# A two-block transformer's mixer: the operand turned without its row scale under the last unit of the feed-forward, the scale put on the columns as they leave, and two narrow products computed by feature

## The reference

```python
def rms_norm(t, g):
    y = tf * lax.rsqrt(jnp.mean(tf * tf, axis=-1, keepdims=True) + NORM_EPS)
    return (y * g)
# first block, layer l
x = x + 0.5 * swiglu(rms_norm(x, ffn1_norm[l]), ffn1_w_in[l], ffn1_w_out[l])
z = rms_norm(x, mix_norm[l]) @ mix_w_in[l]          # 3 attention column groups, 4 forget gates, RWKV columns
z_fox, z_moba, z_rwkv = split(z)
# forgetting attention: s = q k^T / 8 + c_i - c_j, c = cumsum(log_sigmoid(f + bias)), causal softmax
# RWKV: zf = zf + (z_prev - zf) * mu              # mix of a token with the one before it, by feature
#       r, k, v, w_lo, a_lo, g_lo = split(zf); low-rank products of tanh(w_lo), a_lo, sigmoid(g_lo)
# second block, layer l
p = rms_norm_2(x, norm_g[l]) @ w_in[l]              # among its columns: 64 index keys ik and 8 index weights iw
```

## Time and profile before

| | us |
|---|---|
| median of 3 runs | 1896.34 (1893.74 to 1907.27) |
| the profiled execution | 1899.43 |
| its span, first to last instruction | 1898.1 |
| PE busy | 1857.7 (98%) |
| DVE busy | 1165.2 (61%) |
| ACT busy | 927.7 (49%) |
| POOL busy | 93.6 (5%) |
| mean granted clock of TensorE | 0.991 of full speed |

### The profile page before, as it was taken

One profiled execution on the slowest core, in us unless ns is written; L12 is line 12 of the kernel. 1 busy time (PEld: TensorE's weight loads), 2 busy tenths in 40 slices (PEclk: granted clock), 3 DMA queues, 4 the chain that ended last, 5 costly groups with the idle time before them and its releaser, 6 DMA issues.

```text
span 1898.1 us, 28284 instructions
## 1 busy us (share of the span) xinstructions
PE 1857.7 (98%) x11756; PEld 1565.4 (82%) x11756; DVE 1165.2 (61%) x1645; ACT 927.7 (49%) x1409; POOL 93.6 (5%) x59
## 2 busy tenths in 40 slices
PE   7999999999999999999999989999999999999999
PEld 6888888887888888888888878888888888888887
DVE  5555477765655565554677656555588548597556
ACT  5444474234544454445642355444455554556553
POOL 0000010040000000000100400000010000000000
PEclk9999999999999999999999999999999999999999
DMA  6655442023555566554420235655554456454454
GB/s 241 249 183 175 145 156 78 25 79 112 168 189 188 177 191 248 188 176 143 155 71 25 79 111 187 205 184 174 165 168 159 152 188 210 151 166 156 161 186 141
DMA packets 83616, 299.19 MB, mean 158 GB/s; under 512 B 9632, under 2 KB 10784, under 8 KB 83232
## 3 DMA queue, kind: packets, MB, share of 16 engines
q1 hardware_dynamic: 79328, 287.87, 45.8%
q10 hardware_dynamic: 3840, 8.03, 1.2%
q0 software_dynamic: 320, 1.48, 0.2%
HBM read 296.30 MB, written 1.05 MB: 157 GB/s over the span
## 4 chain that ended last, share of the span: by engine, by line
PE 94%; DVE 4%; issue 0%; ACT 0%; DMA 0%; POOL 0%; ACTq 0%; DVEq 0%
PE ps L342 24%; PE ps L344 24%; PE ps L343 24%; PE ps L367 2%; PE ps L369 2%; PE ps L368 2%; PE ps L808 1%; PE ps L1184 1%; PE ps L566 1%; PE ps L1187 1%; DVE wlo L324 1%; PE ps L2500 1%; PE ps L1175 1%; PE ps L1587 1%; PE ps L780 1%; DVE a_lo L420 1%
## 5 line engine op out<-in xcount | busy, mean ns | idle before, releaser
L324 DVE TENSOR_TENSOR wlo<-raw,whi 128x1024 fp32r<-128x1024 f32 (+1 forms) x546 | 663.3, 1222 | 423.0 <-ACT whi L315 422.0
L315 ACT ACTIVATE whi<-raw 128x1024 fp32r<-128x1024 f32 (+1 forms) x546 | 573.0, 1053 | 512.2 <-PE ps L344 468.2
L342 PE MATMUL ps<-whi,a_hi 128*128 128x512 f32 x1696 | 677.0, 399 | 5.8 <-DVE a_lo L1874 1.8
L344 PE MATMUL ps<-whi,a_lo 128*128 128x512 f32 x1696 | 663.8, 391 | 0.0
L343 PE MATMUL ps<-wlo,a_hi 128*128 128x512 f32 x1696 | 662.8, 391 | 0.0
L342 PEld LDWEIGHTS ps<-whi,a_hi 128*128 128x128 f32 x1696 | 320.2, 189 | 76.0 <-DVE a_lo L1874 2.3
L344 PEld LDWEIGHTS ps<-whi,a_lo 128*128 128x128 f32 x1696 | 319.7, 189 | 68.7
L343 PEld LDWEIGHTS ps<-wlo,a_hi 128*128 128x128 f32 x1696 | 320.5, 189 | 62.8
L342 PE MATMUL ps<-whi,h_hi 128*128 128x512 f32 x320 | 124.9, 390 | 0.0
L344 PE MATMUL ps<-whi,h_lo 128*128 128x512 f32 x320 | 124.6, 389 | 0.0
L343 PE MATMUL ps<-wlo,h_hi 128*128 128x512 f32 x320 | 124.5, 389 | 0.0
(11 more groups left out here) (317 smaller groups left out, 1847.3 us busy)
## 6 DMA issues: line engine op xcount, KB each, us to landing
raw<-stream SPq DMA_DIRECT2D x546, 512.0 KB, 3.4
arena<-rows ACTq DMA_DIRECT2D x2, 1026.0 KB, 12.6
arena<-mem ACTq DMA_DIRECT2D x2, 1024.0 KB, 8.7
arena<-lora ACTq DMA_DIRECT2D x2, 768.0 KB, 6.1
arena<-rows ACTq DMA_DIRECT2D x2, 512.0 KB, 4.9
const_tables<-consts POOLq DMA_DIRECT2D x1, 901.0 KB, 4.9
arena<-band POOLq DMA_DIRECT2D x1, 544.0 KB, 4.0
x_res<-x SPq DMA_DIRECT2D x1, 512.0 KB, 3.7
```

Of the source, the lines that this page charges most:

```text
L315: self.split_hi.mark(act.activation(self.weights(self.whi, u), self.weights(self.raw, u), ACT.Copy), u)
L324: self.split_lo.mark(dve.tensor_tensor(self.weights(self.wlo, u), self.weights(self.raw, u), self.weights(self.whi, u).bitcast(F32), ALU.s ...
L342: pe.matmul(out, a_h, hi, start=start, stop=False, skip_group_check=True)
L344: last = pe.matmul(out, a_l, hi, start=False, stop=True, skip_group_check=True)
```

## The change

1. The feed-forward ahead of the mixer now ends as the others do: four pieces are turned unscaled before its last unit, the others between the first two low units. The diagonals and L846 are gone. The first low unit waits for the first tile of `x_done` (bank 1 is being emptied).
2. The row scale is spread over partitions by PE (`pe_mix_spread`, two matmuls into bank 2) and copied by ACT to a tile R. DVE multiplies the low-rank columns and the k, r, v columns with R on their way from PSUM to a tile ZR (which is E2), and the mixes by ACT and DVE read ZR. The attention columns get the scale in the copies they had.
3. The forget gates become features 64 to 67 of the third block: 12 matmuls per unit go, two small transposes behind `pe_rw_lora` come.
4. The index keys of the second block run by feature: 8 x 3 products with 256 moving columns in place of 48 with 72, a copy by ACT, two transposes behind the first unit of `k`, two copies with the scale.
5. In the second tile's forgetting scores the last of the cumulative matmuls leaves out the first 128 columns, where it added zeros.

```diff
     def pe_unit_turned(self, n, blocks, beside=()):
...
-            for out, c, w, first, t in beside:
-                pe.matmul(out, a_h, hi, ...); pe.matmul(out, a_h, lo, ...); pe.matmul(out, a_l, hi, ...)
...
-    def pe_mix_turn(self, l):
+    def pe_mix_spread(self, l):
+        pe.wait_ge(*self.rstd(("mix", l)))
+        pe.wait_ge(*self.x_done(l, "ffn1", 1))
         for t in range(NT):
+            ins = pe.matmul(self.bank(2)[:, t * P:(t + 1) * P], self.rs(0, t).to_broadcast([P, P]), self.c("ident"),
+        self.rw_pe.mark(ins, "rms", l)
+    def act_mix_spread(self, l):
+        act.wait_ge(*self.rw_pe("rms", l))
+        self.rw_act.mark(act.activation(self.R, self.bank(2, S), ACT.Copy), "rms", l)
...
     def dve_rw_low(self, l):
+        dve.wait_ge(*self.rw_act("rms", l))
+            m.mark(dve.tensor_tensor(self.ZR[0:w, i, :], src, self.R[0:w, :], ALU.mult), "scaled", "low", l, i)
+            dve.wait_ge(*self.rw_act("low", l, i))
+            m.mark(dve.scalar_tensor_tensor(y, self.ZR[0:w, i, 0:S - 1], ...), "low", l, i)
+    def dve_rw_scale(self, l, name, unit, bank):
+        dve.wait_ge(*self.unit_used(unit))
+        self.rw_dve.mark(dve.tensor_tensor(self.ZR, src, self.R.unsqueeze(1).to_broadcast([P, 4, S]), ALU.mult),
...
     def pe_mix(self, l):
-        self.pe_mix_turn(l)
         for n in range(4):
             self.pe_rw_low(l, n)
+            if n < 2:
+                self.pe_turn_x(("mix", l), self.TURN_BANKS["mix"], self.x_done(l, "ffn1", 1), 4 + 2 * n, 2)
+        self.pe_mix_spread(l)
...
-                    ins = pe.matmul(out, self.LN[...], self.c("cum")[:, st * S:st * S + nk], ...
+                    ins = pe.matmul(out[:, st * P:nk], self.LN[...], self.c("cum")[:, st * S + st * P:st * S + nk], ...
...
     def pe_unit_keys(self):
+            pe.matmul(out, h, self.AHI[:, kt, :], ...); pe.matmul(out, h, self.ALO[:, kt, :], ...)
+            last = pe.matmul(out, low, self.AHI[:, kt, :], ...)
```

More of the change, by code:

```diff
@@ L623, in act_ffn @@
         self.act_split(4)
[L624 to L625 removed]
+        self.act_early_turn(*self.after_ffn(l, f))
     def dve_h(self, key, j):
@@ L859, in pe_rw_low @@
         pe.wait_ge(*self.turned_lo(("mix", l), 2 * n + 1))
+        if n == 0:
+            pe.wait_ge(*self.x_done(l, "ffn1", 1, "first tile"))
         self.pe_unit_turned(n, [(self.bank(0)[:, S:2 * S], 96, P, True), (self.bank(0)[0:96, 0:S], 0, 96, False),
-                                (self.bank(1)[0:64, 0:S], 224, 64, False)],
-                            [(self.bank(1)[:, S + 4 * t:S + 4 * t + 4], 288, 4, t == 0, t) for t in range(NT)])
+                                (self.bank(1)[0:68, 0:S], 224, 68, True)])
     def pe_rw_cols(self, l, n, banks):
@@ L882, in act_rw_low @@
         act.wait_ge(*self.rw_dve("params", l))
[L883 to L888, removed]
+        for i, w in enumerate((96, P, 68)):
+            act.wait_ge(*self.rw_dve("scaled", "low", l, i))
+            m.mark(act.activation(M[0:w, i, :], self.ZR[0:w, i, :], ACT.Copy, scale=self.pv(PV_OML, i, w)), "low", l, i)
         act.wait_ge(*self.rw_dve("low", l, 0))
@@ L934, in pe_rw_lora @@
         self.rw_pe.mark(ins, "a", l)
+        for t in range(NT):
+            ins = pe.transpose(self.bank(1)[:, S + 4 * t:S + 4 * t + 4], self.LM[64:68, 2, t * P:(t + 1) * P],
+                               self.c("ident")[64:68, 64:68])
+        self.rw_pe.mark(ins, "forget", l)
     def act_rw_lora(self, l):
@@ L1597, in dve_at_scores @@
         dve.wait_ge(*self.at_pe(key, "scores"))
+        if qt and not fox:
+            dve.wait_ge(*self.rw_dve("mixed", "v", l, 3))
         for g in range(2):
@@ L2096, in act_mix @@
         act = self.nc.scalar
+        key, banks, gain, loaded, slot = self.early("mix", l)
         self.act_mix_squares(l)
-        self.act_turn(("mix", l), 8, (4, 5, 6, 7), self.PV[:, PV_MIX:PV_MIX + 8])
+        self.act_turn_x(key, banks, gain, 4, 2)
+        self.act_split(1)
+        self.act_turn_x(key, banks, gain, 6, 2)
         act.wait_ge(self.s_tables, 32)
-        self.act_split(4)
+        self.act_split(2)
+        self.act_mix_spread(l)
+        self.act_split(1)
         self.act_rw_low(l)
@@ L2846, in pe_block2 @@
         self.pe_group(l, "ik", 0)
-        for n in range(3):
-            self.pe_group(l, "k", n)
+        self.pe_group(l, "k", 0)
+        self.pe_keys_turn(l)
+        self.pe_group(l, "k", 1)
+        self.pe_group(l, "k", 2)
         self.pe_sp_index(l)
```

161 lines of the change are left out of this document (89 added, 72 removed).

## The result

| | before | after |
|---|---|---|
| median of executions | 1900.26 us (1893.74 to 1907.27, 4) | 1879.63 us (1878.85 to 1879.87, 4) |
| profiled execution | 1899.43 | 1879.87 |
| its span | 1898.1 | 1878.6 |
| mean granted clock | 0.991 | 0.990 |
| PE busy | 1857.7 | 1840.2 |

The ratio is 0.9898, with an interval of 0.9873 to 0.9923: 1% faster, at the edge of what a measurement of this kernel can tell. The forecast was 1868 and its range ended at 1877, so the time lies 2.6 us above the range. The span fell by 19.5 us where the sum said 28.3. A fourth execution of the kernel before moved its own median from 1896 to 1900.

A forecast was written before the change was run, and what follows sets the result against it. PE's list was taken as the kernel's length (94% of the chain). Gains of 16.6 + 1.0 + 10.7 = 28.3 us took the profiled 1899.43 to 1871.1 and the median from 1896.34 to 1868; range 1860 to 1877.

The forecast's parts named there:

- the sum: All forecast gains together: feed-forward to mixer 16.6, forgetting scores 1.0, index keys 10.7, in all 28.3 us.
- The early turn and the first wait: Ahead of the first low unit: early transposes 0.88, last feed-forward unit 2.7, PE's wait for the residual 1.6 us.
- Low units: Four low units behind the turn, 18 products of 256 columns each: 8.5 us in place of 13.88.
- Spread of the scale, copy, query units, second wait, low-rank products: Behind the low units: spread 0.84, copy of R 0.65, two query units 5.5, wait 0.6, low-rank products 3.73 us.
- Forgetting scores: Second tile, four heads: one product of 128 columns replaces one of 256, gaining 0.4 to 0.5 us a layer, 1 together.
- DVE in the middle: RWKV's three new multiplications a layer on DVE cost PE nothing, bound 1.5 us a layer; chance of DVE bound 0.1.
- Keys: Second block, first key product to indexer's turn: 11.4 us for 16.8 at full clock, gaining 5.4 a layer.
- in the trace each fall ended after 3.5 or 6.9 us: Argument against the mixer staying at half clock for good: falls seen before the change were short.
- a mean clock near 0.996: What the changed profile would show over the kernel; before, the mean granted clock was 0.991.
- a stretch of 3.5 us at half clock: Rival: clock falls at the new waits, slowing low units by 1.5 us a layer, 1871 in all; chance 0.17.
- the rival in which it holds for good: Mixer's small products, feed-forward to cross attention, stay at half clock; 1918 at 100 us more half-clock time; chance 0.03.

The follow-up runs named there:

- the 12 products: Kernel after plus 12 dense 256-column products, results unused, between the values and the second tile's forgetting scores in both layers; median 1880.52 us, ratio 0.9901.
- A shift of 0.9 us: Kernel after plus 8 dense 256-column products, results unused, ahead of layer 0's `pe_mix_spread`; 1877.81 us, ratio 0.9899.
- the 1.9 us in the kernel before: Kernel before plus 16 dense 256-column products, results unused, behind the low units of layer 0; 1905.88 us, ratio 1.0042.
- Dense work put into the row: Kernel after with 12 unused dense products (1880.52 us), or with the third unit of r columns (1875.88 us), put ahead of the second tile's forgetting scores.
- 1.9 us of work put far ahead of it: Kernel after plus 16 dense 256-column products, results unused, ahead of layer 0's `pe_mix_spread`; 1878.03 us, ratio 0.9900.

## Why the prediction was wrong

- **The early turn and the first wait: right.** From the turn's start to the first low unit 5.08 us; forecast 0.88 + 2.7 + 1.6 = 5.2. The wait is 1.27 in both layers, within its bounds, and what ends it is DVE's list, as worked out.
- **Low units: right.** 201.70 to 211.10 is 9.4 with the other half of the turn; forecast 8.5 + 0.9.
- **Spread of the scale, copy, query units, second wait, low-rank products: right, a little dear.** 1.08 for 1.5; a wait of 0.35 for 0.6; 4.0 for 3.9. Together the stretch is 25.6 for 26.1: 17.6 us in both layers where I had 16.6.
- **Forgetting scores: right, under-sized.** 1.7 us in both layers (from the heads at full clock) where I had 1.0.
- **DVE in the middle: right within its bound.** L1161 waits 3.5 for DVE in total, 3.0 before, where I had nothing and a bound of 1.5 a layer.
- **Keys: the size right, the reason half right.** 5.6 a layer for 5.4. I gave the half clock there to the 72-column products; the run without the keys' change shows the same products at full clock in one layer and falling in the other.
- **The step that failed is the one on the clock**: "in the trace each fall ended after 3.5 or 6.9 us", and with it "a mean clock near 0.996" and the rival of "a stretch of 3.5 us at half clock" at the new waits, 3 us in both layers. All of these are one step: the forecast took the half-clock stretches of the trace before as belonging to the instructions under them. So it removed 20.4 of 34.1 us with these, left the other 13.6 where they were, and held all places that ran at full clock to be safe. What the runs showed: 37.6 us after the change, all in the mixers and cross attentions, 13.6 of them in one piece. The terms add up to 17.6 + 1.7 + 11.1 - 0.5 = 29.9; the span fell by 19.5. The remainder, 10.4, is what I put down to the clock; the 11.0 given back between the two places, less the 0.5 of L1161, say the same, and 24 us at half clock can cost up to 12.
- I named the right weakness ("full of small products", "with PE never idle") and put it only under the rival in which it holds for good, 0.03. The moderate form of it, falls of this kind dealt anew over the mixers, was missing. The kernel before alone could have warned of it: its three executions lay 13.5 us apart. Read as time x clock, the forecast's product is 1871.1 x 0.996 = 1863.6, the measured one 1860 to 1861, and over the clocks measured since, 0.984 to 0.996, the forecast's makes a range of 1871 to 1894.
- **The skill's rule on transposes** (the Trainium skill, page "TensorE: Matmul & The Clock Gate", section "Part 4: PE-mode transpose") was what I took as speaking for a fall behind the early turn and the wait. In the trace the clock is 1.00 in the wait and at the low units (200.40 to 207.00), with eight transposes, the last unit's 12 products and 1.27 us of idleness ahead, so this stretch shows no such fall; with that unit in between it is no test of that rule. The same page of the Trainium skill, section "Part 1: The HAM clock gate (the "warmup" mystery)", says that one kernel measures differently from run to run by where the gate's phase stands at its start, and counts the slow start as small. The runs agree that one kernel measures differently, up to 21 us in 1872 with the 12 products in it, more than the whole gain of the change; that the phase is the reason, no run here shows.

What stays open: what exactly decides whether one of the places falls, and so why the kernel after met 37.6 us of it. A shift of 0.9 us, more than 60 us ahead, went with the fall at layer 0's scores gone, but whether the shift or the execution removed it is not separated; only for the 1.9 us in the kernel before do the medians show that the shift cost clock. Dense work put into the row went with a shorter fall or none at the scores in the profiled executions, and so did 1.9 us of work put far ahead of it; the other executions of the same programs, without a trace, show by their mean clock that this does not hold every time. By which part of the row it falls was not separated. What the other executions of the kernel after did is known only by their clock, 0.990 each time.

## What to carry to other kernels

Price an edit in two parts: what it takes from the bounding engine's list at full clock, which could be worked out here to within 2 us of 20 (as time x clock, 18.7 forecast and 20 to 21 measured), and the clock, which no edit owns. For the second, look at time x mean clock over all executions of the kernel before: their spread (16 us here; another of the kernels had 21) is at least the price of a new deal, and it goes into the range of every edit that moves a row of small products, however far ahead it is. A fall that goes away when one suspect is removed convicts nobody until the same edit is seen in a second place, or a mere shift has been tried, and then in more than one execution.

## What the runs showed of the hardware

- TensorE's clock went to 1.2 GHz with PE busy for all of 14.00 us (278.50 to 292.50), at float32 products with 128 and 256 moving columns, and stayed there for 13.6 us; the spread behind them (32 products, L1019) took 3.6 us in place of 1.9. Idleness ahead is not needed: ahead of the falls at 278 and 1026 PE was busy for all of 7 us at full clock. Ahead of the one at 978, in the inverse, it was busy for 4.97 of 6.70.

```profile
271.50:278.50 7.00, 7.00 (x58) 6.60 (x58) 2.95 (x6) 4.17 (x12) 1.38 (x1) 1.00 0.44 150
971.50:978.20 6.70, 4.97 (x107) 4.18 (x99) 6.49 (x15) 3.06 (x10) 0.00 (x0) 1.00 0.01 2
1019.00:1026.00 7.00, 7.00 (x63) 5.41 (x59) 3.65 (x4) 1.24 (x2) 0.00 (x0) 1.00 0.42 136
```

- The turns of probabilities and the values of the cross attention fell to half clock for 3.4 or 6.8 us in both layers of all ten traces.
- 1.27 us of idleness ahead of the first low unit were followed by full clock in both layers; 3.26 before were followed by half.
- One compiled program with the same data (the kernel after with 12 products) varied by 21 us (1871.57 to 1892.71) between executions on one chip, at clocks of 0.996 to 0.984.
- By feature, 24 products with 256 moving columns take 2.82 us (0.118 each), and 48 with 72 moving columns take 5.28 (from 1343.70, without the keys' change: 0.11 each). So a product with 72 moving columns costs about as much as one with 256.
